# A hybrid attention and RWKV-7 decoder step on one core: the chunk part's order written out by hand, and the loads of the second half of the tokens held back

## The reference

```python
x_ext = concat([x_prev_row, x]); proj = x_ext @ w_in          # one projection for both groups of heads
q, k, v = proj[:, 1:, 0:512], ...                             # 8 attention heads of 64
att = dilated_window_attention(q, k_all, v_all, prefix)       # branches (128,1), (512,4), (2048,16), ALiBi
rw = rw_cur + (rw_prev - rw_cur) * mu_shift                   # 8 RWKV-7 heads of 64
def step(S, inp):                                             # for each token, state S is 64 x 64 a head
    sa = einsum('bhvk,bhk->bhv', S, -kk_t)
    S = S * w_t + sa[..., None] * (kk_t * a_t) + v_t[..., None] * k_t
    return S, einsum('bhvk,bhk->bhv', S, r_t)
y_rw = (group_norm(y) + bonus) * g
h = concat([att, y_rw]) @ w_out
x1 = layer_norm(ALPHA * x + h)
f = (silu(causal_conv3(gate)) * up) @ w_ffn_out
y = layer_norm(ALPHA * x1 + f)
```

## Time and profile before

| | |
|---|---|
| median of 3 runs | 838.8 us (837.25 to 838.95) |
| profiled execution | 835.33 us, its span 833.5 us |
| instructions in the span | 21761 |
| TensorE (PE) busy | 796.7 us, 96% |
| VectorE (DVE) busy | 502.2 us, 60% |
| ScalarE (ACT) busy | 326.0 us, 39% |
| GpSimd (POOL) busy | 287.7 us, 35% |
| HBM read, written | 75.34 MB, 5.91 MB |

### The profile page before, as it was taken

How to read it: one execution, slowest core, us unless ns; L and a number is a source line. 1 busy time by engine, 2 the same in 40 slices (tenths; PEclk the granted TensorE clock), 3 DMA queues, 4 the chain that set the end, 5 groups by cost and what they waited for, 6 DMA issues and landing times.

```text
span 833.5 us, 21761 instructions
## 1 busy us (share of the span) xinstructions
PE 796.7 (96%) x9268; PEld 731.2 (88%) x9268; DVE 502.2 (60%) x853; ACT 326.0 (39%) x561; POOL 287.7 (35%) x125
## 2 busy tenths in 40 slices
PE   7999999999998878999999999999999999999996
PEld 5899898898877776789888999999999999999985
DVE  5588867668567667266666886665666662001047
ACT  5543655554413223334264443433333332111134
POOL 0000000000188880327252555454454444444410
PEclk9999999999999999999999999999999999999999
DMA  8222223134262436803121333323323223233303
GB/s 286 87 80 77 76 77 95 59 90 169 66 165 81 127 85 178 238 17 109 61 78 51 102 101 102 101 77 101 99 79 101 84 88 93 91 95 93 110 2 103
DMA packets 32609, 82.85 MB, mean 99 GB/s; under 512 B 5160, under 2 KB 10856, under 8 KB 31872
## 3 DMA queue, kind: packets, MB, share of 16 engines
q1 hardware_dynamic: 32512, 81.46, 31.9%
HBM read 75.34 MB, written 5.91 MB: 97 GB/s over the span
## 4 chain that ended last, share of the span: by engine, by line
PE 89%; DVE 5%; issue 3%; ACT 3%; DMA 1%; POOL 0%; SPq 0%; DVEq 0%; ACTq 0%; POOLq 0%
PE banks L2051 86%; PE banks L2105 1%; DVE z L1324 1%; PE banks L2504 1%; DVE z L1327 1%; DMA att<-in_x 1%; ACT z L1282 1%; ACT z L1294 0%; DVE xx L1324 0%; DVE rw L1324 0%; ACT x L1208 0%; DVE lower L1324 0%; PE banks L2080 0%; ACT z L1213 0%; ACT lsq L1195 0%
## 5 line engine op out<-in xcount | busy, mean ns | idle before, releaser
L729 POOL TENSOR_TENSOR w_lo<-w_raw,w_hi 128x1024 fp32r<-128x1024 f32 (+1 forms) x38 | 97.5, 2566 | 142.7 <-ACT w_hi L864 142.6
L2051 PE MATMUL banks<-x_hi,w_hi 128*128 128x264 f32 x416 | 123.5, 297 | 0.0
L2051 PE MATMUL banks<-x_hi,w_lo 128*128 128x264 f32 x416 | 119.0, 286 | 0.0
L2051 PE MATMUL banks<-x_lo,w_hi 128*128 128x264 f32 x416 | 118.7, 285 | 0.0
L729 POOL TENSOR_TENSOR wx_lo<-w_raw,wx_hi 128x1024 fp32r<-128x1024 f32 (+1 forms) x34 | 87.3, 2567 | 90.0 <-ACT wx_hi L864 89.7
L2051 PE MATMUL banks<-x,w_hi 128*128 128x280 f32 (+1 forms) x544 | 114.2, 317 | 2.5 <-POOL x L805 1.9
L2051 PE MATMUL banks<-x,wx_hi 128*128 128x280 f32 (+1 forms) x544 | 113.3, 316 | 0.0
L2051 PEld LDWEIGHTS banks<-x,w_hi 128*128 128x128 f32 x544 | 91.2, 188 | 8.2 <-POOL x L805 2.4
L2051 PEld LDWEIGHTS banks<-x,wx_hi 128*128 128x128 f32 x544 | 91.2, 188 | 4.9
L2051 PEld LDWEIGHTS banks<-x_hi,w_hi 128*128 128x128 f32 x416 | 78.9, 190 | 10.9 <-issue 10.1
L2051 PEld LDWEIGHTS banks<-x_lo,w_hi 128*128 128x128 f32 x416 | 79.1, 190 | 0.2
(11 more groups left out here) (276 smaller groups left out, 1712.9 us busy)
## 6 DMA issues: line engine op xcount, KB each, us to landing
w_raw<-in_w SPq DMA_DIRECT2D x86, 512.0 KB, 3.5
w_raw<-in_w SPq DMA_DIRECT2D x16, 448.0 KB, 3.3
kv<-in_ck SPq DMA_DIRECT2D x16, 192.0 KB, 3.6
kv<-in_cv SPq DMA_DIRECT2D x16, 192.0 KB, 3.5
att<-in_x SPq DMA_DIRECT2D x8, 264.0 KB, 5.2
att_out<-att SPq DMA_DIRECT2D x1, 2112.0 KB, 9.8
z<-in_xc SPq DMA_DIRECT2D x2, 1040.0 KB, 8.3
y_out<-z SPq DMA_DIRECT2D x8, 260.0 KB, 2.2
```

Source lines behind the costliest of these rows:

```text
L729: pool.tensor_tensor(lo[:, 0:n * P], w_raw[:, s % 2, 0:n * P], hi[:, 0:n * P].bitcast(F32), ALU.subtract)\
L2051: return pe.matmul(out, l, r, start=start, stop=stop)
```

## The change

The diff has two parts.

**Loads of x.** Before SyncE issues the first load of half 1, it now waits until the first load of half 0 has landed. All that stands behind in its queue waits with it.

```diff
         for half in range(2):
+            if half:
+                sp.wait_ge(x_landed[0], 16)
             for q in range(KT // 2):
                 x = slice(half * XH, (half + 1) * XH)
                 sp.dma_start(att[:, 2 * q:2 * q + 2, x], a["x"][:, 2 * q:2 * q + 2, x])\
```

**The order of the chunk part.** Both double loops are replaced by the plain list of their calls, 107 on VectorE and 129 on TensorE. No call is added or dropped and none of the functions changes, so the number of instructions of each engine is the same. These are the calls that stand at another place than before (a shortened diff of the two unrolled lists, calls that keep their order left out):

```diff
 VectorE
 halves(1,3)
-state_sum(0,0)
 update(1,3,0)
 update(1,3,1)
+state_sum(0,0)
 halves(1,4)
 transitions(0)
 state_sum(0,1)
-s_score(2)
 update(1,4,0)
 update(1,4,1)
+s_score(2)
 halves(1,5)
+chain_state(0)
 s_score(3)
-chain_state(0)
...
+halves(2,3)
+s_score(5)
 value_mask(2,1)
-s_score(5)
-halves(2,3)
...
-value_mask(3,0)
 s_shifted()
 halves(3,2)
+value_mask(3,0)
 s_scaled()
 update(3,2,0)
 update(3,2,1)
 value_mask(3,1)
+state_sum(1,0)
 halves(3,3)
-state_sum(1,0)
 state_sum(1,1)
 TensorE
 value_scores(0,1)
+vt_rows(1)
 gathered()
-vt_rows(1)
 full_products(0,1,0)
 full_products(0,1,1)
+half_products(0,2)
 vt_rows(2)
-half_products(0,2)
 full_products(0,2,0)
...
 half_products(1,3)
-step_terms(0)
 full_products(1,3,0)
 full_products(1,3,1)
+step_terms(0)
 half_products(1,4)
...
 half_products(1,5)
+to_tokens(1,0)
 inverse_scores(2,0)
-to_tokens(1,0)
 full_products(1,5,0)
 inverse_scores(2,1)
 chain_step(1)
+to_tokens(1,1)
 full_products(1,5,1)
 start_inverse(2,0)
-to_tokens(1,1)
...
 key_scores(2)
+value_scores(2,0)
 full_products(2,1,0)
 full_products(2,1,1)
-value_scores(2,0)
...
+decode_scores()
 to_tokens(2,2)
-decode_scores()
...
 full_products(3,2,1)
+decode_back()
 value_scores(3,1)
-decode_back()
+step_terms(2)
 half_products(3,3)
-step_terms(2)
 full_products(3,3,0)
+decode_values(0)
 full_products(3,3,1)
 to_tokens(3,0)
-decode_values(0)
...
 value_terms(2)
+half_products(3,5)
 chain_step(4)
 decode_values(1)
-half_products(3,5)
...
 full_products(3,5,1)
+decode_values(2)
 state_outputs(2)
 to_tokens(3,2)
-decode_values(2)
```

More of the change, by code:

```diff
@@ new lines, in _ @@
+        s_score(2)
+        halves(1, 5)
+        chain_state(0)
+        s_score(3)
+        update(1, 5, 0)
+        inverse_start(2, 0)
+        update(1, 5, 1)
+        inverse_start(2, 1)
+        chain_state(1)
+        add_y(0)
+        s_score(4)
+        halves(2, 1)
+        key_masks(2)
+        update(2, 1, 0)
+        update(2, 1, 1)
+        value_mask(2, 0)
+        halves(2, 2)
+        update(2, 2, 0)
+        update(2, 2, 1)
+        halves(2, 3)
+        s_score(5)
+        value_mask(2, 1)
@@ new lines, in _ @@
+        update(2, 3, 0)
+        update(2, 3, 1)
+        halves(2, 4)
+        transitions(1)
+        s_score(6)
+        update(2, 4, 0)
+        update(2, 4, 1)
+        halves(2, 5)
+        chain_state(2)
+        update(2, 5, 0)
+        inverse_start(3, 0)
+        update(2, 5, 1)
+        inverse_start(3, 1)
+        s_score(7)
+        chain_state(3)
+        add_y(1)
+        halves(3, 1)
+        key_masks(3)
+        update(3, 1, 0)
+        update(3, 1, 1)
+        s_shifted()
+        halves(3, 2)
@@ L1681, in attn_sum @@
+        value_mask(3, 0)
+        s_scaled()
+        update(3, 2, 0)
+        update(3, 2, 1)
+        value_mask(3, 1)
+        state_sum(1, 0)
+        halves(3, 3)
+        state_sum(1, 1)
+        update(3, 3, 0)
+        update(3, 3, 1)
+        halves(3, 4)
+        transitions(2)
+        update(3, 4, 0)
+        update(3, 4, 1)
+        halves(3, 5)
+        chain_state(4)
+        update(3, 5, 0)
+        update(3, 5, 1)
+        chain_state(5)
+        add_y(2)
         def attn_sum(t):
@@ new lines, in _ @@
+        inverse_scores(2, 0)
+        full_products(1, 5, 0)
+        inverse_scores(2, 1)
+        chain_step(1)
+        to_tokens(1, 1)
+        full_products(1, 5, 1)
+        start_inverse(2, 0)
+        state_outputs(0)
+        start_inverse(2, 1)
+        to_tokens(1, 2)
+        value_waits(1)
+        half_products(2, 1, lambda h, j: value_side(1, h, j))
+        key_scores(2)
+        value_scores(2, 0)
+        full_products(2, 1, 0)
+        full_products(2, 1, 1)
+        solved_waits(1)
@@ new lines, in _ @@
+        half_products(2, 2, lambda h, j: solved(1, h, j))
+        full_products(2, 2, 0)
+        full_products(2, 2, 1)
+        value_scores(2, 1)
+        half_products(2, 3)
+        step_terms(1)
+        full_products(2, 3, 0)
+        full_products(2, 3, 1)
+        half_products(2, 4)
+        full_products(2, 4, 0)
+        full_products(2, 4, 1)
+        value_terms(1)
+        chain_step(2)
+        half_products(2, 5)
+        inverse_scores(3, 0)
+        to_tokens(2, 0)
+        full_products(2, 5, 0)
@@ new lines, in _ @@
+        inverse_scores(3, 1)
+        chain_step(3)
+        full_products(2, 5, 1)
+        start_inverse(3, 0)
+        to_tokens(2, 1)
+        state_outputs(1)
+        start_inverse(3, 1)
+        decode_scores()
+        to_tokens(2, 2)
+        value_waits(2)
+        half_products(3, 1, lambda h, j: value_side(2, h, j))
+        key_scores(3)
+        full_products(3, 1, 0)
+        full_products(3, 1, 1)
+        value_scores(3, 0)
+        solved_waits(2)
+        half_products(3, 2, lambda h, j: solved(2, h, j))
@@ new lines, in _ @@
+        full_products(3, 2, 0)
+        full_products(3, 2, 1)
+        decode_back()
+        value_scores(3, 1)
+        step_terms(2)
+        half_products(3, 3)
+        full_products(3, 3, 0)
+        decode_values(0)
+        full_products(3, 3, 1)
+        to_tokens(3, 0)
+        half_products(3, 4)
+        full_products(3, 4, 0)
+        full_products(3, 4, 1)
+        value_terms(2)
+        half_products(3, 5)
+        chain_step(4)
+        decode_values(1)
+        to_tokens(3, 1)
@@ L2580, in _ @@
+        full_products(3, 5, 0)
+        chain_step(5)
+        full_products(3, 5, 1)
+        decode_values(2)
+        state_outputs(2)
+        to_tokens(3, 2)
         pe.wait_ge(d_done, 2 * (NLEV - 1) * TB)
```

203 lines of the change are left out of this document (95 added, 108 removed).

## The result

The changed kernel takes 840.6 us in the median of 20 runs against 838.1 for the kernel before in the same comparison. The ratio is 1.0048, with a 95% interval of 1.0031 to 1.0065, so about 4 us slower. The two medians are only 2.5 us apart; I go by the ratio. The forecast was 838.6 us, with 0.45 on no change. The time is inside the range of 835.6 to 841.2; a slowdown clear of its interval is not what was forecast.

What follows compares the result with a forecast made beforehand. TensorE, busy 96% of the span, bounds the kernel, its chunk-part waits mostly for 256-instruction blocks. Start 0, chunk blocks 0 and 3 +0.4 each, s_score(2)'s loads -1.0, the rest 0: -0.2 on 838.8 gives 838.6 us, range 835.6 to 841.2.

Steps and rivals of the forecast that it cites:

- chunk block 3: Last block of the chunk part: reordered VectorE and TensorE calls cost +0.4 us in all, ends 0 and +1.0.
- The start: First microseconds: holding the loads of half 1 is hidden by x's queueing; 0 us, ends -0.3 and +0.5.
- VectorE's order: Chunk block 3: value_mask(3,0) now comes behind the wait for the second group, ahead of update(3,2); +0.45 us.
- Block 0: Chunk block 0: four transposes of vt_rows(2) now stand between half and full products; +0.4 us, ends 0 and +0.6.
- What s_score(2) triggers: Chunk block 1: keys of request 5 load 1.41 us later, shortening the 6.03 us instruction block; -1.0 us, ends -1.8 and +1.4.
- My first rival: Chunk part: the 6.03 us block is freed (-1.8) and one half-clock stretch goes (-1.7); 836.1 us, chance 0.30.
- The basis: Chunk part: TensorE's program loads in 256-instruction blocks, 3.46 us undisturbed; better cover in blocks paced by loading gains nothing.
- the cover I had put first: Chunk block 1: s_score(2) behind update(1,4) covers a TensorE wait of 0.41 us; block booked 0, ends -0.7 and +0.3.
- The rival built on that section: Chunk part: no limit by instruction blocks, so covered xx waits count, at most 2.2 us; 837.4, a little of 0.30.
- the loads of request 5: Chunk block 1, slower rival: these loads land on the instruction block's request, +1.4 us; 841.0 us, chance 0.20.
- The slower start and the third stretch at half clock: First microseconds and chunk part: either one as another way to a slower kernel; chance 0.05.
- my own test: Wrong if chunk-part issue waits change by more than 2 us, or TensorE starts other than 0.3 us around its old time.

Runs made afterwards that it cites:

- e8: Kernel before with TensorE's calls of chunk block 3 alone in the new order; ratio 1.0036 (1.0018 to 1.0053).
- e1: Kernel before with only SyncE's wait on the first load of x added; ratio 1.0019 (0.9998 to 1.0040).
- e4: Kernel before with only VectorE's list of calls from the changed kernel; ratio 1.0022 (1.0000 to 1.0044).
- e11: Kernel before with TensorE's calls of chunk blocks 0 to 2 in the new order; ratio 0.9999 (0.9976 to 1.0021).
- e5: Kernel before with keys of requests 3 to 7 and cached values loaded for 16 rows instead of 96 or 128; ratio 0.9979 (0.9955 to 1.0002).
- e2: Kernel before with TensorE's and VectorE's lists from the changed kernel, without the wait; ratio 1.0076 (1.0046 to 1.0105).
- e13: Kernel before with TensorE's chunk block 3 in the new order, except step_terms(2) stays behind half_products(3,3); ratio 1.0028 (1.0006 to 1.0050).
- e9: Kernel before with one TensorE call moved, step_terms(2) ahead of half_products(3,3); ratio 0.9997 (0.9975 to 1.0019).
- e17: Kernel before with the wait on x, weights 2 issued early and to_tokens(3,1) ahead of half_products(3,5); ratio 1.0004 (0.9988 to 1.0021).
- e6: Changed kernel with the same loads cut to 16 rows as in e5; ratio 1.0008 (0.9988 to 1.0027).
- e18: Changed kernel with weights 2 early, and step_terms(2) and half_products(3,5) back in their old places on TensorE; ratio 1.0035 (1.0018 to 1.0052).
- e16: Changed kernel with weights 2 issued ahead of the two bias loads and the output; ratio 1.0037 (1.0011 to 1.0062).

## Why the prediction was wrong

**The step that failed: chunk block 3, booked at +0.4 us (ends 0 and +1.0).** Of this, +0.45 was for VectorE's order, so TensorE's moves stood at nothing. TensorE's moves alone are 3.0 us (e8, interval 1.5 to 4.4). Three sentences of the working made it small.

- "Moving `step_terms(2)` and one sum of the state ahead of the third level balances itself, since the same instructions stand between the same two points and only their order is another." I had found that the program crosses into a new block every 256 instructions, and then did not ask on which side of a crossing each call lies. The count is the same and the cover is not: +1.7 us in that block with VectorE's old order, +0.7 with the new one, in part given back.
- "`chain_step(4)` and `decode_values(1)` go behind `half_products(3,5)`, where the stall now meets them: 0." It is the other way round. They stood ahead of the stall before, for nothing, and stand behind it now: +0.7 us in that block.
- "-0.1 for a wait at the end that goes, +0.5 if its 128x512 matmuls delay the last `add_y`." I had the right mechanism, and booked none of it. The wait for `yy` came in every kernel with that move, 0.2 to 0.4 us long, and the block is longer by 0.5 us or more.

**The start, booked at 0 with -0.3 and +0.5 as ends.** The first in_product matmul came 0.23 us earlier, near the end of -0.3. For the cost I looked at x's queueing of 1.5 to 2.1 us, which did hide the shift for x, and not at who waits for the last thing behind the wait, weights 2: it was 1.4 us late at its issue, its rounding on VectorE began 2.9 us late (22.20 against 19.29), and TensorE waited 1.27. TensorE reaches the first half products of the chunk part at 221.27 instead of 220.55, a difference within the scatter of that mark. e1 is slower by 0.2%, just not resolved.

**VectorE's order, in my sum only as +0.45 for `value_mask(3,0)`.** e4 has 0.2%, between 0 and 0.4. Where it comes from I can't show. Its blocks of level 3 and behind the stall are those of the kernel before but for a longer stretch at half clock.

**Block 0, +0.4: right.** The block from 225.58 is 4.80 us after and 4.41 before, and the same pair holds in each kernel with and without this move. e11 shows nothing in the time beside it.

**What s_score(2) triggers, -1.0.** The block that took 6.03 us took 5.27, near what I said; but it varies from 4.1 to 6.5 us over the kernels, in both orders, so this proves nothing. My first rival (faster) rested on this term and on one fall of the clock less; the clock went the other way. It was at half for 17.1 us of the chunk part after and 6.8 before, and for 3.4 (e5) to 17.1 (e2, e13) in the others.

**The basis held in part, the use of it didn't.** The issue waits longer than 0.15 us stand at multiples of 256 instructions in every trace, within a few records. But 3.46 us is no fixed pace: from 254 to 268 us the blocks took 3.33 to 4.03 us after. That better cover in the middle of a block is worth nothing is not tested here. The moves didn't give better cover: TensorE's waits for `xx` are 2.1 us (e2) to 4.3 (e9) against 2.2 before, and 3.3 in e11, which has TensorE's covering moves of the early blocks and is at 0.9999. `s_score(2)` behind its update, the cover I had put first, is VectorE's, in e4. The Trainium skill, page "Runtime: NRT & Kernel Launch", section "Instruction fetch mechanics", takes the crossing as mostly hidden. Every trace here disagrees, with 9.7 us (e17) to 19.1 us (e2) of issue waits in the chunk part. The rival built on that section, at 837.4, needed the waits for `xx` to go, and they did not.

The chances were off for the same reason: I gave "slower" 0.20 with the loads of request 5 as its mechanism, and without most of these bytes the larger part of the loss is still there by the point values (e5, e6). The slower start and the third stretch at half clock, which both came in the trace, had 0.05 together. By my own test, that I am wrong if the issue waits of the part change by more than 2 us, the reason was wrong as well: they rose by 4.3 in the traces. That the time still lies within the range is luck: the range reached up to 841.2 for the loads of request 5, not for what took the time.

**What stays open.** How the loss divides within chunk block 3, since the single moves lie within each other's intervals; what VectorE's order costs and where; and why e18 recovers so little. A single trace can't settle these. e16 has every call of the chunk part where the changed kernel has it; its trace has 14.4 us of issue waits and 6.8 us at half clock there, that of the changed kernel 18.4 and 17.1, with ratios of 1.0037 and 1.0048.

## What to carry over

When an engine's program streams in blocks, mark the crossings on its list of calls before you judge a reordering: a move across a crossing changes cover even when nothing is added. The block lengths here suggest that what an engine hands to another belongs ahead of a crossing, and long instructions into the block that waits for its loading anyway; no version gained time by it (e17: 1.0004, e18: 1.0035), so treat it as a reading to test. Compare block lengths only at the same clock. Cost a wait in a DMA queue by its last victim, the load farthest behind it that an engine needs, not by the loads next to it. And where single moves are worth 0.1% and the measurement tells 0.2%, a hand-written order can only be judged as a whole.

## What was unexpected of the hardware

- Cutting the cached keys and values to 16 rows a load left most of the issue waits: from 217 to 350 us still 10.3 us in e5. So most of them are not queueing behind these loads.
- The same block of code is stable to some hundredths of a us where TensorE's own work fills it (5.37 us in five kernels, about 10.7 for the block after the one behind the stall in all), and varies by up to 3 us in front of a stall (the block that ends in the long stall took 5.1 to 7.9 us).
- With the same calls in the chunk part, the changed kernel and e16 spent 17.1 and 6.8 us of it at half clock in their traces. If TensorE was busy all of the difference, that is up to 5 us, half of it, by estimate; the ratios are 0.1% apart.
